# A hybrid decoder step on one core: in the first pair of stick-breaking heads, the merge and the next branch split ahead of the scans, and the weight transposes behind the second branch product

## What is computed

```python
def stick_breaking(q, k, v, sb_bias, q_pos, k_pos):
    z = jnp.einsum('bqhd,bkhd->bhqk', q, k, preferred_element_type=jnp.float32) * (SB_HEAD_DIM ** -0.5)
    z = z + sb_bias.astype(jnp.float32)[None, :, None, None]
    causal = k_pos[None, :] < q_pos[:, None]
    log_keep = jnp.where(causal, jax.nn.log_sigmoid(-z), 0.0)
    log_a = jax.nn.log_sigmoid(z) + lax.cumsum(log_keep, axis=3, reverse=True) - log_keep
    a = jnp.where(causal, jnp.exp(log_a), 0.0)
    return jnp.einsum('bhqk,bkhd->bqhd', a, v.astype(jnp.float32)).astype(v.dtype)
...
    branch = jnp.einsum('btgc,gcd->btgd', ys, w_branch)
    gates = jax.nn.sigmoid(gate_logits.reshape(B, T, N_BRANCH, D_MODEL))
    x1 = x + jnp.sum(gates * branch, axis=2) @ w_o
```

## Time and profile before

| | before |
|---|---|
| median of 3 runs | 1147.26 us (1146.56 to 1147.4) |
| the profiled execution's own time | 1148.54 us |
| span in the trace, first to last instruction | 1146.8 us |
| PE busy | 1066.1 us (93% of the span) |
| DVE busy | 535.9 us (47%) |
| ACT busy | 266.9 us (23%) |
| POOL busy | 153.1 us (13%) |
| bytes moved by DMA | 282.99 MB, mean 247 GB/s |
| mean granted TensorE clock | 0.973 |

### The profile page before, as it was taken

How to read it: one execution, slowest core, us unless ns; L and a number is a source line. 1 busy time by engine, 2 the same in 40 slices (tenths; PEclk the granted TensorE clock), 3 DMA queues, 4 the chain that set the end, 5 groups by cost and what they waited for, 6 DMA issues and landing times.

```text
span 1146.8 us, 15593 instructions
## 1 busy us (share of the span) xinstructions
PE 1066.1 (93%) x6419; PEld 676.4 (59%) x6419; DVE 535.9 (47%) x752; ACT 266.9 (23%) x399; POOL 153.1 (13%) x179
## 2 busy tenths in 40 slices
PE   5999999999996999999993699999999999999995
PEld 5999977988776878996453333333333333333332
DVE  5222224877664556431216144445544554445554
ACT  5322211265445544321202111011110111011100
POOL 0000000012305553000000201111111111111110
PEclk9999999999998999999996699999999999999998
DMA  5622221734541231843109399999999999999931
GB/s 189 239 92 91 76 93 38 238 131 166 170 142 65 93 128 55 304 202 132 59 37 384 142 417 421 428 428 423 426 426 426 427 429 425 425 426 427 425 146 76
DMA packets 50067, 282.99 MB, mean 247 GB/s; under 512 B 6242, under 2 KB 6514, under 8 KB 29524
## 3 DMA queue, kind: packets, MB, share of 16 engines
q1 hardware_dynamic: 41188, 254.78, 55.1%
q0 software_dynamic: 6048, 20.98, 5.2%
q10 hardware_dynamic: 2768, 6.33, 1.5%
HBM read 274.56 MB, written 7.48 MB: 246 GB/s over the span
## 4 chain that ended last, share of the span: by engine, by line
PE 84%; DVE 6%; DMA 3%; POOL 2%; ACT 2%; issue 2%; SPq 0%; DVEq 0%; ACTq 0%; POOLq 0%
PE acc_all L747 25%; PE acc_all L1222 19%; PE acc_all L1236 10%; PE acc_all L877 5%; PE acc_all L1132 5%; PE acc_all L1247 5%; PE acc_all L726 4%; PE acc_all L808 2%; PE acc_all L1250 2%; PE acc_all L927 1%; DMA vals<-in_cache_mem_v 1%; DVE gate_h L2148 1%; DVE act_t L2150 1%; ACT gate_h L1607 1%; POOL beta L400 1%
## 5 line engine op out<-in xcount | busy, mean ns | idle before, releaser
L747 PE MATMUL acc_all<-xn_hi,w_hi 128*128 128x260 f32 x832 | 174.8, 292 | 14.1 <-DVE gate_sb L1832 11.0
L747 PE MATMUL acc_all<-xn_lo,w_hi 128*128 128x260 f32 x832 | 169.0, 285 | 0.0
L747 PE MATMUL acc_all<-xn_hi,w_lo 128*128 128x260 f32 x832 | 168.9, 285 | 0.0
L2159 DVE TENSOR_TENSOR x<-x,acc_all 128x1024 f32<-128x1024 f32 x128 | 152.5, 1214 | 1.8 <-PE acc_all L1247 0.9
L747 PEld LDWEIGHTS acc_all<-xn_hi,w_hi 128*128 128x128 f32 x832 | 130.5, 191 | 23.5 <-DVE gate_sb L1832 13.5
L747 PEld LDWEIGHTS acc_all<-xn_lo,w_hi 128*128 128x128 f32 x832 | 130.3, 191 | 0.0
L747 PEld LDWEIGHTS acc_all<-xn_hi,w_lo 128*128 128x128 f32 x832 | 129.9, 191 | 0.0
L689 POOL TENSOR_SCALAR spread<-tok_row,slots 128x560 fp32r<-128x560 f32 x32 | 54.0, 1687 | 405.0 <-PE acc_all L1250 404.9
L1676 DVE TENSOR_TENSOR w_lo<-w_raw,w_hi 128x1024 fp32r<-128x1024 f32 x52 | 63.4, 1221 | 65.2 <-ACT w_hi L1361 65.0
L2143 DVE COPY up_sb<-acc_all 128x512 f32<-128x512 f32 x32 | 22.1, 692 | 133.2 <-PE acc_all L1223 133.2
L1222 PE MATMUL acc_all<-w_a,xg_t 128*64 128x512 f32 x176 | 80.2, 610 | 0.7 <-ACT xg_t L1596 0.7
(11 more groups left out here) (351 smaller groups left out, 1752.1 us busy)
## 6 DMA issues: line engine op xcount, KB each, us to landing
w_a<-in_w SPq DMA_DIRECT2D x44, 1024.0 KB, 13.1
w_b<-in_w SPq DMA_DIRECT2D x44, 1024.0 KB, 12.9
w_c<-in_w SPq DMA_DIRECT2D x40, 1024.0 KB, 12.6
w_raw<-in_w_in SPq DMA_DIRECT2D x52, 512.0 KB, 3.6
w_a<-in_w SPq DMA_DIRECT2D x11, 2048.0 KB, 14.5
w_b<-in_w SPq DMA_DIRECT2D x11, 2048.0 KB, 14.0
w_c<-in_w SPq DMA_DIRECT2D x10, 2048.0 KB, 14.5
w_br<-in_w_branch SPq DMA_DIRECT2D x24, 256.0 KB, 4.7
```

The lines of the kernel that those rows point to most:

```text
L747: mm = pe.matmul(out[:, a, :], w[:, slot, k, :], x[:, k, a * HALF_TOK:(a + 1) * HALF_TOK], start=first, stop=last)
L2159: dve.tensor_tensor(x1[:, t, :], x1[:, t, :], bank(2 * pair, 2), ALU.add).then_inc(back_ok, 1)
```

## The change

For the first pair of heads alone (h = 0 and 1, steps 8 and 9) three things move:

- On DVE, `merge` of step 8 and `rest_branch` of step 9 come ahead of the pair's scans and weight products, at h = 0. At h = 1 `rest_branch` is then left out, since it is done.
- On ACT, `split_branch` of step 9 comes right behind the survivals, ahead of the decode tokens' exponentials; before it came behind them.
- On PE, the 20 transposes of the pair's weights come behind the branch product of step 9; before they came in front of it, right behind the gate product.

Nothing is added or left out, and the pairs 1 to 3 keep their order.

```diff
--- before.py
+++ after.py
@@ -1053,7 +1053,7 @@
                 if h >= 1:
                     pe.wait_ge(term_ok, h)
                     gate(h, 6)
-                if second:
+                if second and pair >= 1:
                     turn_weights(pair)
                 elif pair >= 1:
                     values(pair - 1)
@@ -1067,6 +1067,7 @@
                 pe.wait_ge(gt_sb, n + 1)
                 branch(n % RING, 1, acc_pair(6)).then_inc(br_ps, 1)
                 if h == 1:
+                    turn_weights(pair)
 
                     pe.wait_ge(zssp_ok, 1)
                     per = NB * HEADS
@@ -1511,11 +1512,14 @@
             for h in range(HEADS):
                 pair, second = divmod(h, 2)
                 n = KD + h
-                if h >= 1:
+                if h >= 2:
                     act.wait_ge(br_ps, n)
                     split_branch(n, n % RING, 1, 16 * (n // RING + 1))
                 if not second:
                     survivals(pair)
+                if h == 0:
+                    act.wait_ge(br_ps, n + 1)
+                    split_branch(n + 1, (n + 1) % RING, 1, 16 * ((n + 1) // RING + 1))
                 if h >= 1:
                     sigmoid(n, 6)
                 if h == 0:
@@ -1961,7 +1965,11 @@
             for h in range(HEADS):
                 pair, second = divmod(h, 2)
                 n = KD + h
-                rest_branch(n, n % RING, 1)
+                if h != 1:
+                    rest_branch(n, n % RING, 1)
+                if h == 0:
+                    merge(n, merged[:, h, :], acc_pair(6))
+                    rest_branch(n + 1, (n + 1) % RING, 1)
                 if not second:
                     runs(pair)
                     weigh(pair)
@@ -1980,7 +1988,7 @@
                             last = dve.tensor_copy(proj[pr, C0 + c, SEQ + PER * g:SEQ + PER * (g + 1)],
                                                    turned[pr, c, :, 2 * c + r])
                     last.then_inc(yt_sb, 1)
-                if h != 6:
+                if h not in (0, 6):
                     merge(n, merged[:, h, :], acc_pair(6))
                 rest_chunk(IN_CHUNKS + n + 2)
                 if h in (2, 4):
```

## The result

| | before | changed |
|---|---|---|
| median | 1147.05 us (4 runs, 1146.56 to 1147.4) | 1138.64 us (4 runs, 1138.25 to 1140.18) |
| ratio, 95% interval | | 0.9929, 0.9917 to 0.9941 |
| the profiled execution's own time | 1148.54 us | 1138.62 us |
| span in the trace | 1146.8 us | 1136.9 us |
| PE busy | 1066.1 us | 1062.0 us |

The change gains 8.4 us of the median; the interval of the ratio stands for 6.8 to 9.5 us. I had forecast 6.9, and a time of 1140.4 within 1139.0 to 1142.6; the median lies 0.36 us under that range. Two later comparisons gave 0.9938 (0.9921 to 0.9955) and 0.9929 (0.9911 to 0.9946).

The account below looks back on a forecast made before the run. PE was taken to bound the kernel, standing still 9.53 us for a merge queued behind unrelated DVE work. Terms -8.67, -1.49 and +3.26 sum to -6.9 us, from 1147.26 to 1140.4 us, range 1139.0 to 1142.6.

Parts of the forecast that it names:

- term 3: End of step 9's gate product to second pair's scores: transposes behind the branch product cost three small waits, +3.26 us.
- term 2: Gate product of step 9: with a short wait in front it takes 5.97 us instead of 7.46, -1.49 us.
- What bounds the kernel: PE bounds most of the span; its 9.5 us stall for the merge of step 8 is where to gain.
- Term 1: PE's stall before the gate product of step 9 shrinks from 9.53 to 0.86 us, -8.67 us.
- My sign of being wrong here: First pair on DVE: scans that last longer than 6.33 us in their new place beside POOL.
- Experts' stage: Rival: the gain is lost in the experts' stage, where DMA share is 1.00; 1147.3 us, no change; chance 5%.
- the slower one: Rival: clock stays low through the whole chain of little waits; 13.5 us slower at most, 1161 us; chance 2%.
- The rival on the clock: Rival: clock falls in the new little waits before the second pair's scores; gain 5.4 us, 1141.9 us; chance 16%.

## Why the prediction was right, and where it was wrong

The mechanism and the sign came as forecast, and each wait where it was forecast; the size was 0.9 us too small on average, and the range too narrow at its fast end. Two terms were mis-sized: the wait for scans and weight products (in term 3) and the low clock (term 2).

- **What bounds the kernel:** right. The stall in front of the gate product of step 9 was the whole matter, and nothing behind it took the gain back but what traces of one kernel differ by. The wait at h = 3 for the decode values that POOL gathers differs from trace to trace: nothing, nothing and 0.7 us before, 0.6, 1.3 and nothing with the change.
- **Term 1, the merge:** -8.67 us forecast and -8.67 measured in the trace that it was forecast from, 0.86 us of wait left. (The prediction has the clock at its low level through the stall; PE stopped at 350.62, and the granted clock was 1.00 from 351 to 353 us and 0.64 from 353 to 355.)
- **Term 2, the clock in the gate product:** -1.49 forecast. Measured 6.01 us against 7.46, 7.81 and 8.14, so -1.45 to -2.13 and -1.8 on average. This term was mis-sized: I took one execution's value for the term and gave it no bounds of its own, though a stall's low clock ends at a different matmul each time. It accounts for 0.3 us.
- **Term 3, the waits that the move uncovers:** +3.26 forecast, +2.61 measured (365.16 - 356.81 = 8.35 us against 5.74). The waits for the sigmoid and for ACT's copies were forecast at 0.85 and 0.9 and measured at 0.78 and 0.96. The step that failed is the one for the scans and weight products: I took 6.33 us between scans and products, and 3.0 us for these, and wrote that masks are no wait any more. But the 6.33 us held such a wait, about 0.2 us between the heads, and some 0.25 us that the scans had paid beside masks. They took 5.89 us, the products, now directly behind each other, 2.86, and the transposes waited 0.47 instead of 1.1 us. The experiment with masks held back brought 0.5 us back: 0.2 as a wait for a mask, the rest in longer scans and products. My sign of being wrong here was scans longer than 6.33 us; shorter ones I had not thought of.
- **Experts' stage:** its loads took nothing back, as I had it: the 610.7, 610.9 and 610.4 us from the partial sums to the end are no longer than before. That rival and the slower one did not come.
- **The rival on the clock, 16%:** it did not come; the clock stayed at 1.00 in all three traces. (It called both rows that it rests on 3 us long; they are 3.90 and 2.35.) What brought the clock down at this place was one long wait, 3.5 and 4.4 us in two experiments, at a cost of 1.3 and 2.9 us. The Trainium skill ("TensorE: Matmul & The Clock Gate", section "Part 4: PE-mode transpose") says that transposes do not count as PE's work in the same way as other matmuls. By that the clock would have been at risk from 360.7 to 365.2 us, over transposes, small sums and two waits. The traces do not agree for these fp32 transposes: the clock stayed at 1.00, and in the experiment with the merge alone it rose while only transposes ran.
- **The total:** the sum of the terms from three traces each is 7.8 us, and the three comparisons give 8.1, 7.1 and 8.1 us by their ratios. Their intervals hold 7.8 (and 6.9). Of the first median's 8.4, the part above 7.8 is within what single executions differ by elsewhere, such as the 1.7 us at the partial sums; where it lies is not shown. My range had reached 1.4 us below the forecast; it had counted the hand-overs and the runs' spread, and not the spread of the low clock, nor a gain from POOL and DVE moving apart. Its bounds were also not added up right: 0.7 us of hand-overs and 0.8 us of spread are 1.5 us, so 1138.9 to 1141.9, where I wrote first 1139.2 to 1141.6 and then 1139.0.

That the branch split of step 9 had to come ahead as well was not tried by itself.

## What to carry to other kernels

When PE waits for one instruction of another engine, look at what stands in front of that instruction, and whether it could start on what is already there: one merge of 0.7 us moved ahead of 9 us of scans and weight products gave two thirds of the gain in its stage. Then fill the wait that the moved work leaves behind with work of the waiting engine that needs only early data, since here the waits under 1 us cost their own length, and those of 3.5 us and more the clock as well. And a duration read where two engines run side by side is not the duration of the same work once they run apart.

## What the runs showed of the hardware

- POOL's 8 masks of 128x128 took 2.85 us mostly ahead of DVE's scans, 5.32 us beside part of them, and 7.21 us beside them in full; 8 scans took 5.96 to 6.41 us. The Trainium skill ("SBUF — State Buffer", section "Who interferes with whom") says that a VectorE instruction with two inputs in SBUF contends with a GpSimd instruction that reads SBUF, and the scans have two such inputs. The traces agree, and show how much: beside the scans one mask of 0.29 us got through for each instruction of DVE, ended 0.1 to 0.15 us behind it, and so took up to 1.2 us beside a scan, while a 512-column scan took 1.24 us instead of 1.19.
- Behind a stall of 9.4 to 9.5 us a gate product took 7.62, 7.97, 8.10 and 8.29 us in four executions, against 6.01 behind a wait of 0.86 us, all read to the end of the last matmul.
- The clock fell in waits of 3.53 and 4.41 us, and did not in four waits of 0.47 to 0.96 us spread over 15 us. Behind the wait of 1.9 us in front of the partial sums it fell in some executions and not in others of the same kernel.
- The clock rose from its low to its high level while PE did nothing but fp32 transposes of 128x128: 0.50 from 361.5 to 364.0 us, 1.00 from 364.4 to 365.0, in the experiment with the merge alone.
